# The exchange of the rotation's halves: four ScalarE copies out of PSUM, or four transfers within SBUF on the product with the sine

## The chip, the cores and the metric

The kernel runs on one core of a Trainium2 chip. The metric is the device time of one execution in microseconds (us), the median of the runs. TensorE (PE) multiplies matrices into the eight PSUM banks, VectorE (DVE) and ScalarE (ACT) do the elementwise work, GpSimd (POOL) splits weights, and SyncE (SP) issues the transfers that bring weights in.

## The reference, cut to what matters

Two blocks run one after the other on 512 positions of width 1024. The first has two layers: differential attention (16 query and key heads of 64 numbers) and windowed attention with grouped keys (16 query heads, 4 key heads), each followed by a gated feed-forward part with a convolution and by a gated embedding. The second block joins a convolution branch with an attention branch. The change touches the rotation of queries and keys in the two attentions of the first block:

```python
def apply_rope(x, cos, sin):
    xf = x.astype(jnp.float32)
    x1, x2 = jnp.split(xf, 2, axis=-1)
    c, s = cos[:, :, None, :], sin[:, :, None, :]
    return jnp.concatenate([x1 * c - x2 * s, x2 * c + x1 * s], axis=-1).astype(x.dtype)
```

Heads lie along partitions, two heads of 64 to a tile of 128 partitions and 512 positions. The halves x1 and x2 of a head are 32 partitions each, so the sine term needs each block of 32 partitions moved to its neighbour's place.

## The kernel before, in words

All matrix products are made three times over (high part by high part, high by low, low by high) from operands split into two parts. Weights come as 328 slabs of 512 KB in a fixed order. For each slab SP loads `raw` (2 slots), ACT copies it to `whi` (4 slots), POOL writes the rest to `wlo` (two instructions), PE uses it for 24 products of 128x512, and `slab_done` lets ACT take the slab four further on (`used`). SP works in order: the load of slab s waits on `lo_ready` until slab s-2 has been split.

Every engine's order is the order in which its code is written. The places of this case are `attention(1)` and `attention(2)`. Each has 32 steps (two heads, one block of 128 queries). In step g:

- PE computes the scores of a later step (`scores`, one step ahead in attention 1, two in attention 2), then a part of a query or key projection (`project_qk`; a tile takes two steps in attention 1, three out of four in attention 2), then the transposes of step g's probabilities, and at every second step the outputs (`outputs`) of the two steps before.
- ACT exponentiates (`exps`) the next step, copies the transposes (`prob_high`), copies a rotated tile (`q_high`), now and then empties the output bank, and where a projection tile has finished takes the next slab (`used`) and exchanges halves (`swap_halves`).
- DVE takes row maxima (`maxima`) of a later step, rotates a tile (`rope`), splits the tile before (`q_low`), normalises the next step (`normalise`), and splits the transposes (`prob_low`).

`swap_halves` (line 1066) makes four ACT copies of 32x512 from the projection's PSUM bank to `swap` (line 1075). `rope` (line 1553) then makes three DVE instructions: PSUM times the cosine table (line 1563, which frees the bank), `swap` times the sine table, both operands in SBUF (line 1564), and the sum, both in SBUF (line 1567). The sine table carries the sign. `rC` and `rS` are the tables, `qraw` and `swap` have two slots each. All of these and the probabilities lie in the buffer `AR`, which is the name that the trace gives. The scores of a new pair of heads wait for `q_ready`, which `q_low` raises. In attention 1 projection tiles alternate between banks 1 and 0. In attention 2 all but the first use bank 0.

In the lines that the profile shows, scores, projections, outputs and norm sums are all PE L495; transposes are PE L719.

Of the kernel before, what the change touches and what calls it, by code (L numbers as in the profile page):

```python
# [187 lines left out]
def build(nc, xT, pT, posd, wts, par, con, lamd, outT):  # L188
    ctx = ExitStack()
    with ctx:  # L190
# [69 lines left out]
        def f32(a):  # L260
# [38 lines left out]
        rcol_ready, rspread = sem("rcol_ready"), sem("rspread")  # L299
        vhi_ready, pad_ready = sem("vhi_ready"), sem("pad_ready")  # L300
        swap_ready, rope_ready, qhi_ready, q_ready = (
            sem("swap_ready"), sem("rope_ready"), sem("qhi_ready"), sem("q_ready"))
# [99 lines left out]

        BEGUN = {1: {}, 2: {-2: 0, -1: 1}, 3: {-2: 2, -1: 3}}
        NPROJ = {1: 14, 2: 8, 3: 8}
# [54 lines left out]
        @block.sync  # L459
        def _(sp):  # L460
            def load(s, slot, freed):
                if freed is not None:

                    sp.wait_ge(lo_ready, freed)
                sp.dma_start(raw[:, slot, :], wts[s]).then_inc(raw_ready[slot], 16)

            for s in range(4):
                load(s, s % RAWS, s - 1 if s >= RAWS else None)
            with sp.Fori(1, SLABS // 4) as i:
                for j in range(4):  # L470
                    load(4 * i + j, j % RAWS, 4 * i + j - 1)
            for m in range(KC):

                bank, before = tile_of("down2.2", m // 4, m % 4)
                sp.wait_ge(tile_free[bank], before + 2)
                sp.dma_start(outT[:, m, :], X[:, m, :]).then_inc(out_stored, 16)
            sp.wait_ge(out_stored, 16 * KC)
# [498 lines left out]
        def _(act):  # L976
# [89 lines left out]
            def swap_halves(stage, t, n):  # L1066

                if stage not in ("qk1a", "kq2a"):
                    used(stage, 0, t)
                bank, _ = tile_of(stage, 0, t)  # L1070
# [76 lines left out]
            def attention(kind):  # L1147
# [6 lines left out]
                for g in range(steps):  # L1154
# [26 lines left out]
                    if done is not None and kind < 3:  # L1181
                        swap_halves(PROJ[kind], done, place_of(kind, done)[0])
                    if done is not None and kind == 3:
# [103 lines left out]
            values("v1", (1,), 4, T)  # L1287
            swap_halves("qk1", 0, 2)
            q_high(*place_of(1, 0))
            attention(1)  # L1290
# [18 lines left out]
            values("v2", (0,), 0, 256)  # L1309
            swap_halves("kq2", 0, QT0[2] + 2)  # L1310
            exps(2, 0)
            q_high(*place_of(2, 0))
            swap_halves("kq2", 1, QT0[2] + 3)
            attention(2)
# [139 lines left out]
        def _(dve):  # L1454
# [98 lines left out]
            def rope(stage, t, n):  # L1553
# [3 lines left out]

                dve.wait_ge(swap_ready, n + 1)

# [6 lines left out]
                dve.wait_ge(tile_free[bank], before + 2)  # L1566
                tt(qraw[:, b, :], qraw[:, b, :], swap[:, b, :], ALU.add).then_inc(rope_ready, 1)

            def q_low(n, b, which):
# [92 lines left out]
            def attention(kind):  # L1662
# [8 lines left out]
                for g in range(steps):  # L1671
# [5 lines left out]
                    if kind == 3:  # L1677
                        taps(TAPS_A_STEP[g % 4])
                    if kind < 3 and begun is not None:
                        rope(PROJ[kind], begun, place_of(kind, begun)[0])  # L1680
                    if kind < 3 and halfway is not None:
# [16 lines left out]
                    if g + 1 < steps:  # L1698
                        normalise(kind, g + 1)
                    prob_low(kind, g)  # L1700
                    if kind == 2:
                        for c in OSPLIT.get(g, ()):
# [157 lines left out]
            values_low("v1", (1,), T)  # L1860
            rope("qk1", 0, 2)
            q_low(*place_of(1, 0))
            attention(1)
# [16 lines left out]
            for t in range(2):  # L1880
                q_low(QT0[2] + t, 0, 1 - t)
            values_low("v2", (0,), 256)
            maxima(2, 0)
            rope("kq2", 0, QT0[2] + 2)
            attention(2)
# [377 lines left out]
```

## Time and profile before

| What | Value |
|---|---|
| Median of 3 runs | 2182.42 us (2181.17 to 2186.17) |
| The profiled execution's own time | 2183.27 us |
| Its span (first to last instruction) | 2181.3 us |
| Busy: PE, DVE, ACT, POOL | 2081.8, 1251.8, 975.4, 912.7 us |
| Mean granted TensorE clock | 0.977 of full speed |
| Copies of 32x512 by ACT (line 1075) | 104, at 30.9 to 914.9 us |

The profile's times are microseconds from the span's start. In a timeline a row says when an instruction began, how long it (or a run of equal ones) took, and in brackets how long its engine sat idle just before and what released it. Attention 1 runs from about 86 to 262 us, attention 2 from about 784 to 945 us. The row of a PE instruction's length is modelled; the distance between the starts of successive rows is what it costs.

### The profile page before, as it was taken

Reading aid. Unit: us, or ns where it says so; the run is one execution under the profiler, and the core shown is the slowest. Engines: PE = TensorE matmul, PEld = TensorE weight load, DVE = VectorE, ACT = ScalarE, POOL = GpSimd, SP = SyncE. Lnnn points to the kernel's source line nnn. Section 1 sums busy time; section 2 is a strip of 40 time slices with the busy share of each in tenths; the row PEclk is TensorE's granted clock in tenths of the full one; section 3 lists DMA queues with packets and bytes.
Section 4 is the critical chain, followed back from the end, with each engine's and each line's share of the span. In section 5 each row is a group of like instructions: output and inputs, shape, how many; then the busy total and the mean of one; then the engine's idle time right before and its main releaser. Section 6 shows DMA issues by size and latency. Waiting matters only on the chain. (4 is left out here: it accounts for less than half of the span.)

```text
span 2181.3 us, 28619 instructions
## 1 busy us (share of the span) xinstructions
PE 2081.8 (95%) x9896; PEld 1696.5 (78%) x9896; DVE 1251.8 (57%) x1830; ACT 975.4 (45%) x1546; POOL 912.7 (42%) x660
## 2 busy tenths in 40 slices
PE   6999899999999989899999999999979999999999
PEld 5777578888887877778888887777768688888887
DVE  7477756636265668866726357548779664313222
ACT  5577534524245466644524245434642434423222
POOL 4422034545545431134555456344105354445444
PEclk9999799999999989999999999999989999999999
DMA  4211022323223210012222323222102222332223
GB/s 152 78 49 49 20 66 96 100 97 96 97 97 112 82 58 30 30 49 94 99 97 96 100 93 116 87 78 78 40 11 97 77 87 96 97 97 96 96 97 106
DMA packets 49923, 179.53 MB, mean 82 GB/s; under 512 B 5536, under 2 KB 5792, under 8 KB 49824
## 3 DMA queue, kind: packets, MB, share of 16 engines
q1 hardware_dynamic: 48384, 174.09, 24.2%
q10 hardware_dynamic: 1440, 4.08, 0.5%
q8 instruction: 68, 1.11, 0.2%
q14 instruction: 31, 0.25, 0.0%
HBM read 176.05 MB, written 2.10 MB: 82 GB/s over the span
## 5 line engine op out<-in xcount | busy, mean ns | idle before, releaser
L487 POOL TENSOR_TENSOR wlo<-raw,whi 128x512 fp32r<-128x512 f32 x656 | 912.5, 1414 | 1254.2 <-ACT whi L982 1252.8
L495 PE MATMUL PS<-Bhi,whi 128*128 128x512 f32 x2368 | 936.9, 396 | 29.2 <-POOL wlo L487 14.9
L495 PE MATMUL PS<-Blo,whi 128*128 128x512 f32 x2368 | 926.8, 391 | 0.0
L495 PE MATMUL PS<-Bhi,wlo 128*128 128x512 f32 x2368 | 926.7, 391 | 0.0
L982 ACT ACTIVATE whi<-raw 128x1024 fp32r<-128x1024 f32 x328 | 345.8, 1057 | 591.8 <-PE PS L495 521.8
L495 PEld LDWEIGHTS PS<-Bhi,whi 128*128 128x128 f32 x2368 | 447.6, 189 | 139.8 <-issue 30.1
L495 PEld LDWEIGHTS PS<-Bhi,wlo 128*128 128x128 f32 x2368 | 447.4, 189 | 94.8
L495 PEld LDWEIGHTS PS<-Blo,whi 128*128 128x128 f32 x2368 | 448.0, 189 | 90.7 <-issue 0.5
L1465 DVE TENSOR_TENSOR AR<-PS,R 128x512 f32<-128x512 f32 x172 | 116.5, 689 | 241.0 <-PE PS L495 228.9
L1517 DVE TENSOR_TENSOR X<-X,PS 128x512 f32<-128x512 f32 x96 | 65.8, 687 | 232.6 <-PE PS L495 231.8
L1722 DVE SCALAR_TENSOR_TENSOR AR<-AR,par_sb 128x511 f32<-128x511 f32 x88 | 117.0, 1329 | 8.8 <-ACT AR L1205 8.8
L1220 ACT ACTIVATE Bhi<-AR 128x512 f32 x66 | 41.8, 633 | 166.7 <-DVE AR L1738 166.7
L1940 DVE SCALAR_TENSOR_TENSOR AR<-AR,par_sb 128x512 f32<-128x512 f32 x120 | 114.6, 1012 | 0.0
L1725 DVE SCALAR_TENSOR_TENSOR AR<-AR,par_sb 128x511 f32<-128x511 f32 x88 | 106.8, 1213 | 12.9 <-DVE AR L1722 2.9
L1095 ACT ACTIVATE AR<-PS,nmax 128x512 f32<-128x512 f32 (+3 forms) x160 | 93.3, 590 | 42.7 <-DVE nmax L1584 40.7
L1474 DVE SCALAR_TENSOR_TENSOR Blo<-X,par_sb,Bhi 128x512 fp32r<-128x512 f32 x56 | 65.1, 1163 | 40.2 <-ACT Bhi L1003 39.9
L1205 ACT ACTIVATE AR<-AR,par_sb 128x512 f32<-128x512 f32 x88 | 71.0, 807 | 38.5 <-DVE AR L1465 38.5
L1116 ACT ACTIVATE pthi<-PS 128x512 fp32r<-128x512 f32 (+3 forms) x128 | 56.6, 477 | 67.0 <-PE PS L719 66.0
L1481 DVE TENSOR_TENSOR acc<-acc,sq 128x512 f32<-128x512 f32 x64 | 85.1, 1330 | 0.0
L1742 DVE TENSOR_TENSOR Blo<-AR,Bhi 128x512 f32 x66 | 47.1, 714 | 61.5 <-ACT Bhi L1220 61.5
L719 PE MATMUL PS<-constR,AR 128*128 128x128 f32 x368 | 62.0, 300 | 18.6 <-DVE ptlo L1633 13.1
L719 PEld LDWEIGHTS PS<-constR,AR 128*128 128x128 f32 x368 | 46.8, 153 | 39.7 <-DVE AR L1625 17.2
(222 smaller groups left out, 2072.8 us busy)
## 6 DMA issues: line engine op xcount, KB each, us to landing
raw<-in_weights SPq DMA_DIRECT2D x328, 512.0 KB, 3.3
X<-in_xT ACTq DMA_DIRECT2D x4, 512.0 KB, 7.7
out<-X SPq DMA_DIRECT2D x8, 256.0 KB, 3.2
AR<-in_pT ACTq DMA_DIRECT2D x2, 512.0 KB, 3.9
par_sb<-in_parameters ACTq DMA_DIRECT2D x1, 322.0 KB, 4.5
AR<-in_positions ACTq DMA_DIRECT2D x1, 256.0 KB, 9.0
con_sb<-in_constants ACTq DMA_DIRECT2D x1, 206.5 KB, 8.8
AR<-in_lambdas ACTq DMA_DIRECT2D x1, 128.0 KB, 8.7
```

Source lines behind the costliest of these rows:

```text
L487: ins = pool.tensor_tensor(wlo[:, j, c], raw[:, j % RAWS, c], f32(whi[:, j, c]), ALU.subtract)
L495: return pe.matmul(out, w, x, start=start, stop=stop)
L719: last = pe.transpose(PS[:, 2 + n % 2, k * P:k * P + P], source[:, k * P:k * P + P], ident)
L982: act.activation(whi[:, slot, :], raw[:, slot % RAWS, :], ACT.Copy)\
L1095: act.activation(probs(kind)[:, 2 * (g % 2) + s, 0:nb * P], PS[:, score_bank(kind, n), 0:nb * P], ACT.Exp, bias=nmax[:, n % 4:n % 4 + 1], ...
L1205: act.activation(cv[:, 2 * pair + u, :], us[:, 2 * pair + u, :], ACT.Identity, scale=conv_w[:, l, 1, u, bass.ds(q, 1)], bias=conv_w[:, l, ...
L1465: tt(out, PS[:, bank, :], R[:, :], ALU.mult).then_inc(tile_free[bank], 1)
L1481: tt(acc[:, :], acc[:, :], sq[:, slot, :], ALU.add).then_inc(sq_used, 1)
L1517: tt(X[:, m, :], X[:, m, :], PS[:, bank, :], ALU.add)\
L1722: own.step(stt(c[:, 1:T], x[:, 0:T - 1], conv_w[:, l, 0, u, bass.ds(q, 1)], c[:, 1:T], ALU.mult, ALU.add))
L1725: stt(c[:, 0:T - 1], x[:, 1:T], conv_w[:, l, 2, u, bass.ds(q, 1)], c[:, 0:T - 1], ALU.mult, ALU.add).then_inc(conv_done, 1)
L1940: ins = stt(out, src, k, out, ALU.mult, ALU.add)
```

## The change

The tiles `qk1a` and `kq2a` (the first two of each attention) keep the old way. For the 22 others (14 in attention 1, 8 in attention 2) `swap_halves` and `rope` are gone. ACT does only `used`. DVE multiplies PSUM by the sine table into `qraw` (`rope_sin`, in the step in which the projection finishes, after `prob_low`). SP exchanges the halves of that product from `qraw` to `swap` with four transfers of 32x512 (`exchange`), placed in its program ahead of the load of the slab six further on. A step later DVE multiplies PSUM by the cosine table into the same `qraw` and subtracts `swap` (`rope_add`, after `normalise` and ahead of `prob_low`). SP's loop over slabs is written out for the groups of four that hold such an exchange. In attention 1 the first tile's `rope_add` and `q_high` move into step 0.

```diff
+            def exchange(n):
+
+                sp.wait_ge(sin_ready, n - 1 if n < QT0[2] else n - 3)
+
+                sp.wait_ge(rope_ready, n - 1)
+                for to, of in ((0, 32), (32, 0), (64, 96), (96, 64)):
+                    sp.dma_start(swap[to:to + 32, n % 2, :], qraw[of:of + 32, n % 2, :])\
+                        .then_inc(exchanged[n % 2], 16)
+
+            ahead = {SLAB0["qk1"] + j + 6: j + 2 for j in range(NPROJ[1])}
+            ahead.update({SLAB0["kq2"] + j + 6: QT0[2] + 2 + j for j in range(NPROJ[2])})
...
+                    for s in range(4 * at, 4 * at + 4):
+                        if s in ahead:
+                            exchange(ahead[s])
+                        load(s, s % RAWS, s - 1)
...
-        BEGUN = {1: {}, 2: {-2: 0, -1: 1}, 3: {-2: 2, -1: 3}}
+        BEGUN = {1: {-1: 0}, 2: {-2: 0, -1: 1}, 3: {-2: 2, -1: 3}}
...
                     if done is not None and kind < 3:
-                        swap_halves(PROJ[kind], done, place_of(kind, done)[0])
+                        used(PROJ[kind], 0, done)
...
+            def rope_sin(stage, t, n):
+
+                done(stage, 0, t)
+                bank, _ = tile_of(stage, 0, t)
+
+                dve.wait_ge(q_ready, n - 1)
+                dve.wait_ge(qhi_ready, n - 1)
+                tt(qraw[:, n % 2, :], PS[:, bank, :], rS, ALU.mult).then_inc(sin_ready, 1)
+
+            def rope_add(stage, t, n):
+                bank, before = tile_of(stage, 0, t)
+                b = n % 2
+
+                dve.wait_ge(exchanged[b], 64 * (n // 2 if n < QT0[2] else n // 2 - 1))
+                tt(qraw[:, b, :], PS[:, bank, :], rC, ALU.mult).then_inc(tile_free[bank], 1)
+                dve.wait_ge(tile_free[bank], before + 2)
+                tt(qraw[:, b, :], qraw[:, b, :], swap[:, b, :], ALU.subtract).then_inc(rope_ready, 1)
...
-                    if kind < 3 and begun is not None:
-                        rope(PROJ[kind], begun, place_of(kind, begun)[0])
                     if kind < 3 and halfway is not None:
                         q_low(*place_of(kind, halfway))
...
                     if g + 1 < steps:
                         normalise(kind, g + 1)
+                    if kind < 3 and begun is not None:
+                        rope_add(PROJ[kind], begun, place_of(kind, begun)[0])
                     prob_low(kind, g)
+                    if kind < 3 and finished(kind, g) is not None:
+                        t = finished(kind, g)
+                        rope_sin(PROJ[kind], t, place_of(kind, t)[0])
...
             values("v1", (1,), 4, T)
-            swap_halves("qk1", 0, 2)
-            q_high(*place_of(1, 0))
+            used("qk1", 0, 0)
             attention(1)
...
-            rope("qk1", 0, 2)
-            q_low(*place_of(1, 0))
+            rope_sin("qk1", 0, 2)
             attention(1)
...
+            rope_sin("kq2", 0, QT0[2] + 2)
             maxima(2, 0)
-            rope("kq2", 0, QT0[2] + 2)
+            rope_add("kq2", 0, QT0[2] + 2)
+            rope_sin("kq2", 1, QT0[2] + 3)
             attention(2)
```

ACT at the start of attention 1, before: the row of line 982 is the last `used` ahead of it, line 1095 is `exps`, line 1116 `prob_high`, line 1081 `q_high`.

```order
L1063 ACTIVATE Bhi1<-PS,rcol 128x512 x4
L982 ACTIVATE whi<-raw 128x1024 [waits raw_ready0,slab_done]
L1075 ACTIVATE AR<-PS 32x512 [waits rope_ready]
L1075 ACTIVATE AR<-PS 32x512 x3
L1081 ACTIVATE qkhi<-AR 128x512 [waits rope_ready]
L1095 ACTIVATE AR,sum1<-PS,nmax 128x512 [waits max_ready]
L1095 ACTIVATE AR,rsum<-PS,nmax 128x512 [waits max_ready]
L1116 ACTIVATE pthi<-PS 128x4x128 [waits trans_done]
```

The same place in the changed kernel, where its own lines are 1007 (`used`), 1118 (`exps`), 1139 (`prob_high`) and 1104 (`q_high`):

```order
L1088 ACTIVATE Bhi1<-PS,rcol 128x512 x4
L1007 ACTIVATE whi<-raw 128x1024 [waits raw_ready0,slab_done]
L1118 ACTIVATE AR,sum1<-PS,nmax 128x512 [waits max_ready]
L1118 ACTIVATE AR,rsum<-PS,nmax 128x512 [waits max_ready]
L1139 ACTIVATE pthi<-PS 128x4x128 [waits trans_done]
L1104 ACTIVATE qkhi<-AR 128x512 [waits rope_ready]
```

The first exponentials of attention 1's loop no longer stand behind the four copies and the `q_high` of the first tile.

DVE in attention 2, before: from the `prob_low` (line 1633) of the step in which a tile finishes to the `q_low` (line 1571) two steps on. Lines 1581, 1592 and 1596 are `maxima`, lines 1610 to 1625 `normalise`.

```order
L1633 TENSOR_TENSOR ptlo<-PS,pthi 128x2x128 [waits pthi_ready] x2
L1581 TENSOR_REDUCE nmax<-PS 128x1 [waits score_done] x2
L1592 TENSOR_TENSOR nmax<-nmax,nsink 128x2 [waits dve_step]
L1596 TENSOR_TENSOR sdiff<-nmax,nsink 128x2 [waits max_ready]
L1563 TENSOR_TENSOR AR<-PS,AR 128x512 [waits qhi_ready,q_ready,swap_ready]
L1564 TENSOR_TENSOR AR<-AR 128x512
L1567 TENSOR_TENSOR AR<-AR 128x512 [waits tile_free0,dve_step]
L1610 TENSOR_TENSOR rsum<-rsum 128x2 [waits sink_ready,exp_ready]
L1621 RECIPROCAL rinv<-rsum 128x2 [waits dve_step]
L1625 TENSOR_SCALAR AR<-AR,rinv 128x384 [waits dve_step]
L1625 TENSOR_SCALAR AR<-AR,rinv 128x384
L1633 TENSOR_TENSOR ptlo<-PS,pthi 128x2x128 [waits pthi_ready] x2
```

The same stretch of the changed kernel (line 1673 `prob_low`, 1598 `rope_sin`, 1621 to 1636 `maxima`, 1650 to 1665 `normalise`, 1605 and 1607 `rope_add`):

```order
L1673 TENSOR_TENSOR ptlo<-PS,pthi 128x2x128 [waits pthi_ready] x2
L1598 TENSOR_TENSOR AR<-PS,AR 128x512 [waits qhi_ready,q_ready,slab_done]
L1621 TENSOR_REDUCE nmax<-PS 128x1 [waits score_done] x2
L1632 TENSOR_TENSOR nmax<-nmax,nsink 128x2 [waits dve_step]
L1636 TENSOR_TENSOR sdiff<-nmax,nsink 128x2 [waits max_ready]
L1650 TENSOR_TENSOR rsum<-rsum 128x2 [waits sink_ready,exp_ready]
L1661 RECIPROCAL rinv<-rsum 128x2 [waits dve_step]
L1665 TENSOR_SCALAR AR<-AR,rinv 128x384 [waits dve_step]
L1665 TENSOR_SCALAR AR<-AR,rinv 128x384
L1605 TENSOR_TENSOR AR<-PS,AR 128x512 [waits exchanged1]
L1607 TENSOR_TENSOR AR<-AR 128x512 [waits tile_free0]
L1673 TENSOR_TENSOR ptlo<-PS,pthi 128x2x128 [waits pthi_ready] x2
```

There are still three full instructions for a tile. One moved ahead of `maxima`, two moved behind `normalise`, and the instruction that frees bank 0 is now among these two.

SP in the changed kernel, where before a loop held only loads (line 477 is `exchange`, line 466 `load`):

```order
L466 DMA raw<-in_weights 128x1024
L493 REGISTER_ALU
L493 COMPARE_AND_BRANCH
L477 DMA AR<-AR 32x512 [waits rope_ready,sin_ready]
L477 DMA AR<-AR 32x512 x3
L466 DMA raw<-in_weights 128x1024 [waits lo_ready]
```

Each load of these stretches now stands behind four transfers that wait for DVE.

## Rows read from the trace of the kernel before

**Rows 1.** The page, busy time of the engines over the span.

```profile
PE 2081.8 (95%) x9896; PEld 1696.5 (78%) x9896; DVE 1251.8 (57%) x1830; ACT 975.4 (45%) x1546; POOL 912.7 (42%) x660
```

**Rows 2.** Windows: stretch, length, busy us (instructions) by engine, PEclk, DMA share, GB/s.

```profile
95.00:100.00 5.00, 5.00 (x15) 3.49 (x15) 3.70 (x8) 4.92 (x11) 2.52 (x2) 0.66 0.01 3
...
93.00:231.00 138.00, 135.38 (x705) 99.34 (x703) 105.84 (x202) 106.95 (x213) 31.99 (x26) 0.99 0.14 47
231.00:262.00 31.00, 23.94 (x85) 13.28 (x86) 23.69 (x41) 17.97 (x38) 0.86 (x1) 0.80 0.05 17
799.00:921.00 122.00, 109.87 (x740) 91.79 (x740) 101.97 (x286) 75.54 (x223) 15.18 (x12) 0.93 0.10 31
```

**Rows 3.** Timeline of PE at the start of attention 1.

```profile
94.73 0.49 PE L495 MATMUL PS<-qkhi 64*128 64x512 f32 x1 [1.42 <-ACT AR L1095]
```

**Rows 4.** Timeline of ACT at the start of attention 1.

```profile
87.43 2.39 ACT L1075 ACTIVATE AR<-PS 32x512 f32<-32x512 f32 x4
...
93.90 0.69 ACT L1095 ACTIVATE AR<-PS,nmax 128x512 f32<-128x512 f32 x1 [1.36 <-DVE nmax L1584]
```

**Rows 5.** Timeline of DVE in the middle of attention 1.

```profile
151.90 1.29 DVE L1584 TENSOR_REDUCE nmax<-PS 128x1 f32<-128x512 f32 x2 [0.54 <-PE PS L495]
153.57 0.69 DVE L1563 TENSOR_TENSOR AR<-PS,AR 128x512 f32<-128x512 f32 x1 [0.39 <-ACT AR L1075]
...
165.71 0.69 DVE L1563 TENSOR_TENSOR AR<-PS,AR 128x512 f32<-128x512 f32 x1 [2.48 <-ACT AR L1075]
```

**Rows 6.** Timeline of ACT near the end of attention 1's projections.

```profile
234.44 1.28 ACT L1138 ACT_TABLE_LOAD   x1
...
237.64 0.69 ACT L1095 ACTIVATE AR<-PS,nmax 128x512 f32<-128x512 f32 x1
```

**Rows 7.** Timeline of DVE in attention 2, around one finished tile.

```profile
855.52 1.02 DVE L1581 TENSOR_REDUCE nmax<-PS 128x1 f32<-128x384 f32 x2
856.64 0.70 DVE L1592 TENSOR_TENSOR nmax<-nmax,nsink 128x2 f32<-128x2 f32 x1
857.38 1.21 DVE L1596 TENSOR_TENSOR sdiff<-nmax,nsink 128x2 f32<-128x2 f32 x1
858.50 0.68 DVE L1563 TENSOR_TENSOR AR<-PS,AR 128x512 f32<-128x512 f32 x1
...
860.42 0.15 DVE L1610 TENSOR_TENSOR rsum<-rsum 128x2 f32<-128x2 f32 x1
...
861.48 0.75 DVE L1633 TENSOR_TENSOR ptlo<-PS,pthi 128x256 fp32r<-128x256 f32 x2
...
863.19 0.16 DVE L1596 TENSOR_TENSOR sdiff<-nmax,nsink 128x2 f32<-128x2 f32 x1
863.27 0.68 DVE L1571 SCALAR_TENSOR_TENSOR qklo<-AR,qkhi 128x512 fp32r<-128x512 f32 x1
```

**Rows 8.** Timeline of ACT, the same place.

```profile
855.98 2.40 ACT L1075 ACTIVATE AR<-PS 32x512 f32<-32x512 f32 x4
```

**Rows 9.** Timeline of POOL, the same place.

```profile
856.03 2.53 POOL L487 TENSOR_TENSOR wlo<-raw,whi 128x512 fp32r<-128x512 f32 x2 [16.43 <-ACT whi L982]
```

**Rows 10.** Timeline of PE in attention 2.

```profile
801.54 0.76 PE L495 MATMUL PS<-Bhi,whi 128*128 128x512 f32 x1
...
859.12 0.38 PE L495 MATMUL PS<-qkhi 64*128 64x256 f32 x1 [0.94 <-ACT AR L1095]
...
860.41 0.67 PE L495 MATMUL PS<-Bhi,whi 128*128 128x512 f32 x1
...
883.20 0.39 PE L495 MATMUL PS<-qkhi 64*128 64x256 f32 x2 [1.11 <-DVE qklo L1571]
```

**Rows 11.** Transfers by SP: the stores of 256 KB, issue and landing; three issues on the timeline.

```profile
DMA to landing us min/median/max: 2.0/3.2/4.6
...
2159.94 1.33 SPq L476 DMA_DIRECT2D out<-X  x3
```

More of the change, by code:

```diff
@@ L300, in build @@
         vhi_ready, pad_ready = sem("vhi_ready"), sem("pad_ready")
+        sin_ready, exchanged = sem("sin_ready"), [sem(f"exchanged{n}") for n in range(2)]
         swap_ready, rope_ready, qhi_ready, q_ready = (
@@ L468, in _ @@
                 load(s, s % RAWS, s - 1 if s >= RAWS else None)
-            with sp.Fori(1, SLABS // 4) as i:
-                for j in range(4):
-                    load(4 * i + j, j % RAWS, 4 * i + j - 1)
+            def exchange(n):
[6 more added lines that the diff above has]
+            ahead.update({SLAB0["kq2"] + j + 6: QT0[2] + 2 + j for j in range(NPROJ[2])})
+            groups = sorted({s // 4 for s in ahead})
+            at = 1
+            while at < SLABS // 4:
+                if at in groups:
+                    for s in range(4 * at, 4 * at + 4):
+                        if s in ahead:
+                            exchange(ahead[s])
+                        load(s, s % RAWS, s - 1)
+                    at = at + 1
+                else:
+                    end = min([x for x in groups if x > at] + [SLABS // 4])
+                    with sp.Fori(at, end) as i:
+                        for j in range(4):
+                            load(4 * i + j, j % RAWS, 4 * i + j - 1)
+                    at = end
             for m in range(KC):
@@ L1066, in swap_halves @@
             def swap_halves(stage, t, n):
-                if stage not in ("qk1a", "kq2a"):
-                    used(stage, 0, t)
                 bank, _ = tile_of(stage, 0, t)
@@ L1309, in _ @@
             values("v2", (0,), 0, 256)
-            swap_halves("kq2", 0, QT0[2] + 2)
+            used("kq2", 0, 0)
             exps(2, 0)
             q_high(*place_of(2, 0))
-            swap_halves("kq2", 1, QT0[2] + 3)
+            used("kq2", 0, 1)
             attention(2)
@@ L1556, in rope @@
                 b = n % 2
-                dve.wait_ge(swap_ready, n + 1)
+                dve.wait_ge(swap_ready, n + 1 if n < 2 else n - QT0[2] + 3)
                 if n >= 2:
```

## The prediction

> **What bounds the kernel now.** I began with the page: TensorE is busy for 95% of the span [rows 1], so a microsecond counts only if TensorE idles for it or runs it at the low clock. Windows over the two attentions came next, since nothing else is edited. In attention 1's projections (93 to 231 us) TensorE is busy for 135.4 of 138 us, after them for 23.9 of 31 us at a clock of 0.80, and in attention 2 (799 to 921 us) for 109.9 of 122 us at 0.93 [rows 2]. So attention 1 has almost nothing to give while it projects, and attention 2 has 12 us of idle time. Last came the waits of TensorE in each place, and the timelines of ScalarE and VectorE around them.
>
> At the start of attention 1 TensorE waits 1.42 us for exponentials [rows 3]. ScalarE starts these only at 93.90, because the four copies (2.39 us from 87.43) and the first tile's rotation stand in front [rows 4]. The clock then falls: the window 95 to 100 has 0.66 of full speed [rows 2], a mixture of 2.4 and 1.2 GHz after an idle spell.
>
> In the middle of attention 1 VectorE waits 0.39 and 2.48 us for the copies, in turn [rows 5], and TensorE does not wait with it.
>
> In attention 2 each finished tile shows two idle spells of TensorE: 0.94 us for exponentials that stand behind the copies, and 1.11 us for `q_low` [rows 8, 10]. The second depends on VectorE alone, which has no gap from 855.52 to 863.27 [rows 7].
>
> **What is removed from ScalarE.** 22 tiles times four copies, 2.4 us a tile [rows 4, 8], 53 us in all. By the windows ScalarE is not the bound, so most of it is worth nothing. It is worth time in the places above.
>
> *Start of attention 1.* The scores of the next step are done ahead of 91 us, and `exps` follows them at once instead of at 93.90. The 1.42 us should vanish, and with it the fall of the clock: 5 us times 0.34, or 1.7 us. Sum 3.1 us. The lower bound is 0 (another release, VectorE's, comes just as late), the upper 3.8.
>
> *End of attention 1's projections.* The exponentials at 237.64 come behind two table loads, the first at 234.44 [rows 6], and these follow the `q_high` of the last tile. That still waits for the rotation, which now stands behind `normalise`. I take 0, between a loss of 0.3 and a gain of 1.7.
>
> **What is moved on VectorE.** Three full instructions a tile remain (0.6 us each from start to start), so its work does not shrink, but their places change.
>
> *Attention 2, a middle tile* (`g` is the step after the one that finishes it). `rope_sin` comes ahead of `maxima`: 855.5 to 856.1. `maxima` then ends at 857.1. Its two tiny instructions take 0.70 and 1.21 us where they take 0.16 elsewhere [rows 7], and they end at 858.50, when POOL's 2.53 us from 856.03 end [rows 9]. So they should still end at about 858.55, and the sine product has gone in for nothing. What is behind them shrinks by 0.6 us: `normalise` (860.42 to 861.48, so 1.06 us), two instructions of `rope_add`, `prob_low`, `maxima`, `q_low`. `q_low` starts near 862.75 instead of 863.27. The cost: bank 0 is freed behind `normalise`, at 858.55 + 1.06 + 0.6 = 860.2, while TensorE began the next projection at 860.41 [rows 10]. That just fits. Net, 0.5 us for each of the 6 tiles that finish inside the loop, 3.0 us. Bounds: 0 if the tiny instructions slip by the 0.6 us, 2.05 a tile if both spells went.
>
> The Trainium skill ("SBUF — State Buffer", Who interferes with whom) says that a VectorE instruction with two SBUF inputs is shut out by a GpSimd instruction that reads SBUF, and one with a PSUM input is not. The two stretched rows agree with it, and by it the sum stays as it is.
>
> *Attention 2, first tiles.* There `rope` followed `maxima` at once and the next projection started at 801.54 [rows 10]. Now `q_low` (0.6) and `normalise` (1.06) come in between, so it starts up to 1.6 us later. TensorE had about a microsecond of waits right behind it, which covers some. I book a loss of 1.0, between 0 and 1.6.
>
> *Middle of attention 1.* VectorE is busy for 105.8 of 138 us over 13 tiles, which leaves 2.5 us of idle time a tile [rows 2]. `normalise` now waits for the exponentials (about 0.9 us in one step, 0.3 in the other) with no rotation to cover it. That leaves 1.3 us a tile. The outputs wait for `prob_low`, now behind `rope_add`, but by the steps' pace (11 us a tile) it is done some 2 us ahead. I take 0.
>
> **What is added on SyncE.** 88 transfers of 64 KB, 22 times four. The trace of before has no transfer within SBUF and none this small. The nearest are the stores of 256 KB: three issues take 1.33 us, 0.44 each, and one lands 2.0 us after its issue at the least, 3.2 in the median [rows 11]. So the fourth lands 3 x 0.44 + 2.0 = 3.3 us after the sine product, at the median 4.5. I take 3.3, because a quiet queue is the nearest row and the piece is a quarter of it.
>
> The cover in attention 2 is `maxima` to 858.55 and `normalise`: 856.1 to 859.6, 3.5 us. In attention 1 it is `maxima` 1.2, the wait 0.9 and `normalise` 1.1, so 3.2 us, and 1.3 spare. If the fourth lands L us after the product, attention 2 pays 6 x (L - 3.5) and attention 1 pays 13 x (L - 4.5). At 3.3 both are nothing. Queued behind `exchange` on SP is the load of the slab six further. It waits anyway for POOL's split, 2.5 us after ScalarE's copy of the slab, and both start at the same `slab_done`; the four issues end about when that does, and a slab then has a whole tile's time (11 to 19 us) to land. No cost.
>
> **The sum.** 3.1 + 0 + 3.0 - 1.0 + 0 = 5.1 us. The profiled execution took 2183.27 us (span 2181.3 and 2.0 around it), 0.9 above the median of 2182.42, so the profile should come to 2178.2 and the median to 2177.3 us.
>
> **The rivals.**
>
> *The exchange arrives late (slower).* VectorE, which works in order, stands at `rope_add` with `prob_low` and the next `maxima` behind it. The sum turns at L = 4.35: 6 x 0.85 = 5.1. At 4.9 it gives 8.4 + 5.2 - 5.1, 8.5 us slower, 2191. For it speaks the stores' median of 3.2; against it that those queue behind one another and behind loads, and that they are four times as large. The Trainium skill ("SBUF — State Buffer", Can I just issue two DMAs to hit both halves?) says that transfers to separate groups of partitions serialize. If each of the four took a full 2.0 us after the other, L would be 8 and the kernel 67 us slower; but three stores issued within 1.33 us with a largest landing of 4.6 do not look so [rows 11]. Chance 0.2 for slower.
>
> *The gain is lost again in attention 2 (same).* With L between 3.8 and 4.5, or bank 0 freed after TensorE wants it by 0.5 us a tile, its 3.0 us go and the first tiles still cost 1.0. What remains is 3.1 - 1.0 = 2.1: 2180.3 us. A longer single gap can also bring the clock down, 1.7 us each time. For it speaks how closely 860.2 stands to 860.41. Chance 0.3.
>
> *More than forecast.* If the clock of attention 2 (0.93 over 122 us, 8.5 us lost) gains from fewer gaps, some 5 us more: 2172. It is in the forecast's chance.
>
> **Numbers.** Forecast 0.5, its own range 2172 to 2178. A measurement of this kernel tells about 0.2%, or 4.4 us, from no change, so faster means below 2178.0. Faster 0.5, same 0.3, slower 0.2. The range runs from 2171 to 2191.
>
> **What would show it.** Right: no idle spell at TensorE before the third pair of scores of attention 1 and a full clock behind it; ScalarE's `exps` right behind `maxima`; no idle time at `rope_add` for a transfer; `q_low` of attention 2 half a microsecond nearer to its tile's end; landing of the 64 KB transfers near 2.0 us. Wrong: VectorE idle at line 1605 with a transfer as releaser, issues of more than 0.44 us, TensorE waiting for bank 0 at a projection, or a new wait of transposes for `prob_low`.

## The result, and the profile after

The changed kernel took 2189.23 us in the median of 8 runs (2182.72 to 2195.50), the one before 2182.14 us in 8 runs beside it (2179.72 to 2186.27). The ratio is 1.0026, with a 95% interval from 1.0016 to 1.0037: about 6 us slower by the ratio, 7 between the medians, where 2177.3 us and faster was forecast. The profiled execution took 2189.8 us (span 2187.8).

The page, busy time of the engines: ScalarE lost the forecast 53 us of work [rows 1], and the kernel is slower all the same.

```profile
PE 2084.4 (95%) x9896; PEld 1701.2 (78%) x9896; DVE 1253.0 (57%) x1830; ACT 922.8 (42%) x1458; POOL 912.8 (42%) x660
```

Windows of the same stretches as [rows 2]:

```profile
95.00:100.00 5.00, 5.00 (x24) 3.75 (x24) 4.93 (x9) 3.12 (x7) 2.99 (x2) 1.00 0.23 56
93.00:231.00 138.00, 134.80 (x724) 99.85 (x723) 113.91 (x210) 79.93 (x167) 33.34 (x26) 1.00 0.25 75
231.00:262.00 31.00, 26.66 (x86) 15.60 (x85) 24.30 (x42) 16.73 (x36) 0.00 (x0) 0.61 0.00 1
799.00:921.00 122.00, 106.02 (x720) 90.10 (x719) 91.65 (x264) 56.37 (x185) 15.16 (x12) 0.91 0.12 36
```

The start of attention 1 came out as forecast: in 95 to 100 us the clock is 1.00 instead of 0.66. Attention 2 is where the kernel is worse: TensorE is busy for 106.0 of 122 us instead of 109.9, at 0.91 instead of 0.93.

TensorE and ScalarE at the start of attention 1, in place of [rows 3, 4]: ScalarE's exponentials start at 90.56 instead of 93.90, and the scores at 93.11 wait for nothing.

```profile
93.11 0.50 PE L520 MATMUL PS<-qkhi 64*128 64x512 f32 x2
```

```profile
90.56 0.69 ACT L1118 ACTIVATE AR<-PS,nmax 128x512 f32<-128x512 f32 x1 [3.28 <-DVE nmax L1624]
```

The waits of TensorE over the whole kernel (total us, times, longest). The first row is new, and it is bank 0: line 1605 is the cosine product that frees it. The last row was 11.4 us before.

```profile
PE PS L520 <- DVE AR L1605: 17.2, 6, 3.4
...
PE PS L520 <- ACT AR L1118: 2.6, 2, 1.7
```

Around one tile of attention 2, VectorE, in place of [rows 7] (1598 `rope_sin`, 1621 to 1636 `maxima`, 1665 `normalise`, 1605 and 1607 `rope_add`, 1611 `q_low`):

```profile
854.24 0.68 DVE L1598 TENSOR_TENSOR AR<-PS,AR 128x512 f32<-128x512 f32 x1
854.84 1.01 DVE L1621 TENSOR_REDUCE nmax<-PS 128x1 f32<-128x384 f32 x2
...
857.68 0.75 DVE L1665 TENSOR_SCALAR AR<-AR,rinv 128x384 f32<-128x384 f32 x2
859.51 0.69 DVE L1605 TENSOR_TENSOR AR<-PS,AR 128x512 f32<-128x512 f32 x1 [1.08 <-DMA AR<-AR]
...
862.64 0.69 DVE L1611 SCALAR_TENSOR_TENSOR qklo<-AR,qkhi 128x512 fp32r<-128x512 f32 x1
```

SyncE's queue there, and the summary of all 88 transfers (issue time min/median/max in ns; then us to landing):

```profile
854.95 3.09 SPq L477 DMA_DIRECT2D AR<-AR  x4
858.08 0.58 SPq L466 DMA_DIRECT2D raw<-in_weights  x1
```

```profile
L477 SPq DMA_DIRECT2D AR<-AR x88: 507/591/2050, 86.9 to 918.7; - x88
...
DMA to landing us min/median/max: 1.9/2.0/3.8
```

TensorE there, in place of the 860.41 of [rows 10]:

```profile
860.35 0.47 PE L520 MATMUL PS<-Bhi,whi 128*128 128x512 f32 x1 [2.66 <-DVE AR L1605]
```

The landing of 2.0 us was right. The issue was not: 0.59 us in the median, and the four of this tile take 3.09 us (the second of them alone 1.27). The sine product ends at about 854.9, the fourth transfer lands just ahead of 859.51: L is 4.6 us, not 3.3. VectorE stands still for 1.08 us, and TensorE for 2.66.

**Two yardsticks.** The profile's executions differ by some us in stages that no kernel here touches, so I also read each place by itself, from the starts of ScalarE's copies of weight slabs (there are 328 in a fixed order). *Stretch* is the time from the copy of the 115th slab to that of the 127th, which holds all of attention 2. *Period* is the time from one projection tile of its middle to the next. Before: stretch 190.0 us (766.3 to 956.3), period 19.0 to 19.3. After: 197.2 us (763.0 to 960.2), period 20.2 to 21.0:

```profile
853.69 1.06 ACT L1007 ACTIVATE whi<-raw 128x1024 fp32r<-128x1024 f32 x1
873.92 1.06 ACT L1007 ACTIVATE whi<-raw 128x1024 fp32r<-128x1024 f32 x1
894.63 1.06 ACT L1007 ACTIVATE whi<-raw 128x1024 fp32r<-128x1024 f32 x1
```

So the changed kernel is 3.3 us ahead when it comes to attention 2 (763.0 against 766.3), and 3.9 behind when it leaves it.

The stretch is the coarser yardstick. Its last part, from the 126th copy to the 127th, comes when the last tile has been projected, and takes 43.8 to 47.4 us in the kernels below (without e6_split and e7_double) though only the last tile's rotation is left in it. With one profile of each kernel, stretches that lie less than 3 us apart show little. So the table also has the time from the 121st copy to the 126th, which is five periods.

### The profile page after: what moved, and what is told of

The parts are those of the page before. It is cut to its first block and busy times, and to the rows that moved or that the text cites. A ratio compares the mean times of both kernels' runs of the same rounds, so it can differ in the third digit from the quotient of the medians.

```text
span 2187.8 us, 28555 instructions
## 1 busy us (share of the span) xinstructions
PE 2084.4 (95%) x9896; PEld 1701.2 (78%) x9896; DVE 1253.0 (57%) x1830; ACT 922.8 (42%) x1458; POOL 912.8 (42%) x660
## 3 DMA queue, kind: packets, MB, share of 16 engines
q8 instruction: 68, 1.11, 0.2%
## 5 line engine op out<-in xcount | busy, mean ns | idle before, releaser
L520 PE MATMUL PS<-Bhi,whi 128*128 128x512 f32 x2368 | 936.4, 395 | 47.0 <-DVE AR L1605 17.2
L1785 DVE TENSOR_TENSOR Blo<-AR,Bhi 128x512 f32 x66 | 47.1, 714 | 61.5 <-ACT Bhi L1243 61.5
```

The lines of the kernel that those rows point to most:

```text
L520: return pe.matmul(out, w, x, start=start, stop=stop)
```

## The experiments

All ratios are to the kernel before, with their 95% intervals.

| Kernel | Ratio | Stretch, us | Period, us | 121st to 126th copy, us |
|---|---|---|---|---|
| before | 1 | 190.0 | 19.0 to 19.3 | 95.3 |
| changed | 1.0026 (1.0016 to 1.0037) | 197.2 | 20.2 to 21.0 | 102.7 |
| e1_att1 | 0.9989 (0.9975 to 1.0003) | 189.6 | 19.0 to 19.2 | 95.2 |
| e2_att2 | 1.0042 (1.0026 to 1.0058) | 195.8 | 19.1 to 21.6 | 101.1 |
| e3_nodma | 0.9986 (0.9974 to 0.9997) | 189.7 | 18.4, the last 19.2 | 92.7 |
| e4_earlycos | 1.0018 (1.0005 to 1.0030) | 196.1 | 20.4 to 20.6 | 102.5 |
| e5_latesub | 1.0039 (1.0025 to 1.0053) | 196.1 | 20.3 to 20.7 | 102.2 |
| e6_split | 1.0217 (1.0200 to 1.0234) | 213.0 | 22.0 to 23.5 | 112.6 |
| e7_double (two runs) | 1.0275 (1.0255 to 1.0295) | 217.7 | 23.4 to 24.0 | 118.4 |
| e8_cos_nodma | 0.9970 (0.9959 to 0.9981) | 187.8 | 18.24 | 91.2 |
| e9_sinfirst | 0.9983 (0.9973 to 0.9993) | 185.9 | 18.2 to 18.4, the first 19.8 | 93.0 |
| e10_delay | 1.0004 (0.9995 to 1.0014) | 194.4 | 20.5 to 20.7, the first 19.0 | 101.2 |
| e11_traffic | 0.9983 (0.9973 to 0.9994) | 185.9 | 18.2 to 18.4, the first 19.8 | 92.9 |
| e12_after_sinfirst | 1.0000 (0.9989 to 1.0010) | 189.5 | 18.4 to 19.4 | 94.4 |

### Each attention alone

e1_att1: attention 2 goes back to the copies and `rope`.

```diff
-            ahead.update({SLAB0["kq2"] + j + 6: QT0[2] + 2 + j for j in range(NPROJ[2])})
```

> The exchange by transfers is kept in attention 1 alone (14 tiles); attention 2 is as in the kernel before. Theory (the loss lies wholly in attention 2, where the one bank for projection tiles is freed too late, while the start of attention 1 gains what was forecast): the second step of scores in attention 2 begins at about 780.8 us against 784.1 before, attention 2 takes what it took before, and the whole is 2.5 to 4 us faster than the kernel before (ratio about 0.9985). Rival (the transfers slow every place they are used in, through the longer issues on SyncE or through the traffic): also slower than before, ratio 1.000 or above.

e2_att2: attention 1 goes back to them.

```diff
-            ahead = {SLAB0["qk1"] + j + 6: j + 2 for j in range(NPROJ[1])}
```

> The exchange by transfers is kept in attention 2 alone (8 tiles); attention 1 is as in the kernel before. Theory: TensorE waits 2.6 to 3.4 us at each of six projection tiles for bank 0, attention 2 is 9 to 10 us longer, ratio to the kernel before about 1.0043. Rival (loss spread over both places): about half of the changed kernel's loss, ratio 1.001 to 1.002.

Attention 1 alone gives 0.9989, in the median 2 us faster, though the interval just holds 1. Attention 2 alone gives 1.0042, as expected, with a stretch 5.8 us longer where 9 to 10 were expected. The loss lies in attention 2. That attention 1 gains is shown better by its own pace: two of its projection tiles take 22.0 us from copy to copy in the kernel before and in e2_att2, and 20.9 to 21.2 in the changed kernel and in e1_att1 (the first pair apart). More on this below.

### Without transfers, in the same places

e3_nodma: `exchange` and the wait for it are left out.

```diff
-                dve.wait_ge(exchanged[b], 64 * (n // 2 if n < QT0[2] else n // 2 - 1))
```

> The changed kernel without its 88 transfers and without VectorE's waits for them; the exchange of halves is left out, so that swap holds what it held, and all else stays in its place. It separates the place of the instructions from the time of the transfers. Theory (in attention 2 both count: of a bank wait of 2.66 us about 1.1 is the late transfer, about 1.6 the place of the cosine product behind normalise): the bank wait falls to about 1.6 us a tile, but does not go, and the kernel is 5 to 8 us faster than the changed kernel, 0 to 2 us faster than the one before. Rival A (only the transfers' lateness matters): no bank wait is left and the kernel comes to about the forecast, 2177 us or less. Rival B (only the place matters, and the transfer is hidden in it): within 2 us of the changed kernel.

TensorE in e3_nodma, the same tile. The bank wait is 1.46 us, as expected, and `q_low` costs another 0.74.

```profile
856.07 0.47 PE L509 MATMUL PS<-Bhi,whi 128*128 128x512 f32 x1 [1.46 <-DVE AR L1593]
...
857.53 0.82 PE L733 MATMUL PS<-constR,AR 128*128 128x128 f32 x6
859.09 0.39 PE L509 MATMUL PS<-qkhi 64*128 64x256 f32 x2 [0.74 <-DVE qklo L1599]
```

The stretch is 189.7 us, 0.3 below the kernel before and 7.5 below the changed one. But the 0.3 hides two things. Up to the 126th copy e3_nodma is 3.1 us faster than the kernel before, 2.7 of it in the five periods. Then its last part takes 47.1 us instead of 44.3, and e8_cos_nodma has 47.4 there; in both the granted clock is 0.66 in the window 935 to 945 us, and 0.83 in the kernel before. So placement alone does gain while tiles are projected. The transfers then cost 10.0 us in five periods (102.7 against 92.7), 2.0 a tile.

The wait does not account for that. TensorE idles 2.66 us a tile in the changed kernel, and 1.46 + 0.74 = 2.20 in e3_nodma. Most of the rest is the clock, 0.91 in 860 to 880 us of the changed kernel and 1.00 there in e3_nodma. In the changed kernel the products behind the long wait start 0.23 us apart at first, then 0.42:

```profile
861.61 0.63 PE L520 MATMUL PS<-Bhi,wlo 128*128 128x512 f32 x1
862.03 1.48 PE L744 MATMUL PS<-constR,AR 128*128 128x128 f32 x6
863.45 0.59 PE L520 MATMUL PS<-qkhi 64*128 64x256 f32 x2
```

### Bank 0 freed early

e4_earlycos: `rope_cos`, right behind `maxima` in attention 2, frees the bank; `rope_add` is only the subtraction.

```diff
+            def rope_cos(stage, t, n):
+                bank, before = tile_of(stage, 0, t)
+                tt(sq[:, n % 2, :], PS[:, bank, :], rC, ALU.mult).then_inc(tile_free[bank], 1)
...
+                    tt(qraw[:, b, :], sq[:, b, :], swap[:, b, :], ALU.subtract).then_inc(rope_ready, 1)
```

> In attention 2 the cosine product goes into a buffer of its own (sq, free there) right behind maxima, where the rotation stood before, and frees bank 0 there; only the subtraction waits for the transfers, behind normalise. Transfers and their number are as in the changed kernel. Theory: TensorE's waits for bank 0 in attention 2 (six of 2.6 to 3.4 us) go, VectorE still idles about 0.5 to 1 us a tile for the transfer and q_low is no earlier than in the kernel before, so attention 2 comes back to about its time before, and with the gain of attention 1 the kernel is 2 to 5 us faster than the one before. Rival (the late transfer itself holds the chain through q_low and the probabilities, whatever the bank does): less than 3 us faster than the changed kernel, still at or above the one before.

My theory failed here, and the rival came true. The waits for bank 0 shrank from 17.2 to 3.0 us, and the stretch by only 1.1. VectorE idles just 0.59 us a tile for the transfer, ahead of the subtraction:

```profile
855.97 0.69 DVE L1611 TENSOR_TENSOR AR<-sq,AR 128x512 f32<-128x512 f32 x1 [0.59 <-DMA AR<-AR]
```

TensorE now waits in other places of the same chain, 1.04 us for `prob_low` and 1.12 for `q_low`:

```profile
857.14 0.85 PE L744 MATMUL PS<-constR,AR 128*128 128x128 f32 x6 [1.04 <-DVE ptlo L1682]
859.11 0.56 PE L520 MATMUL PS<-qkhi 64*128 64x256 f32 x2 [1.12 <-DVE qklo L1620]
```

e8_cos_nodma is e4_earlycos without transfers.

> The kernel with the cosine product behind maxima in attention 2, without its 88 transfers and without the waits for them; the exchange of halves is left out. With the kernel without transfers before it, it gives the price of the cosine product's place where no transfer is late. Theory: no waits for bank 0 and none for transfers, the stretch between the 115th and 127th slab copies is 187 to 189 us, against 189.9 without transfers in the place of the changed kernel: the place is worth 1 to 3 us. Rival (place is worth nothing, VectorE's chain is as long either way): 189.5 to 190.5.

Its stretch is 187.8 us, 8.3 below e4_earlycos, and its five periods are 11.3 us shorter. Six tiles with 0.59 us of idle time are 3.5 us. So lateness costs more than its length, or the transfers cost in another way too.

### Subtraction later, and two queues

e5_latesub moves the subtraction behind `prob_low`.

```diff
+                    prob_low(kind, g)
+                    if kind == 2 and begun is not None:
+                        rope_add(PROJ[kind], begun, place_of(kind, begun)[0])
```

> As the last one (cosine product into a buffer of its own behind maxima in attention 2), and the subtraction there moved behind prob_low, so that the transfers have about a microsecond more to land. Theory now (in attention 2 TensorE follows VectorE's chain, and what counts is the time in which VectorE stands and waits for the fourth transfer; where the bank is freed is a lesser part): VectorE waits for no transfer in attention 2, the stretch between the copies of the 115th and the 127th weight slab by ScalarE, 190.0 us before and 197.2 in the changed kernel, is 188 to 190.5, and the kernel is 2 to 4 us faster than the one before. Rival (the transfers cost by more than their wait, for instance by slowing other work): it stays at 194 us or more, slower than before.

Within attention 2's loop VectorE waits for a transfer for 0.3 us in all (and 2.3 once ahead of it), and the stretch stays at 196.1. Another miss. TensorE now meets one spell of 1.87 us, and the projection behind it takes 3.52 us (840.05 to 843.57), against 2.19 for the same nine products in e8_cos_nodma (858.48 to 860.67):

```profile
838.79 0.38 PE L520 MATMUL PS<-qkhi 64*128 64x256 f32 x1 [1.87 <-DVE qklo L1620]
...
840.05 0.79 PE L520 MATMUL PS<-Bhi,whi 128*128 128x512 f32 x1
```

e6_split issues two of each tile's four transfers from ScalarE.

```diff
+            def exchange_act(n):
+                act.wait_ge(sin_ready, n - 1 if n < QT0[2] else n - 3)
+                act.wait_ge(rope_ready, n - 1)
+                for to, of in ((64, 96), (96, 64)):
+                    act.dma_start(swap[to:to + 32, n % 2, :], qraw[of:of + 32, n % 2, :])\
+                        .then_inc(exchanged[n % 2], 16)
```

> The changed kernel with two of each tile's four transfers issued by ScalarE and two by SyncE, side by side; nothing else moves. If the issues (0.59 us each, one after the other) are the late part, the fourth lands 1.2 us earlier, VectorE's wait of 1.08 us at rope_add in attention 2 goes, TensorE's wait for bank 0 falls from 2.7 to about 1.6 us and the stretch between the 115th and 127th slab copies from 197.2 to about 191 us; the kernel is 4 to 7 us faster than the changed one. Rival (the two queues still complete one after the other, or ScalarE's own issues delay its exponentials by as much): less than 2 us faster.

It is 2.2% slower. ScalarE works in order: it waits for the sine product and issues for 1.87 us, and its slab copy and the exponentials stand behind that.

```profile
864.44 1.87 ACTq L1105 DMA_DIRECT2D AR<-AR  x2
866.41 1.06 ACT L1007 ACTIVATE whi<-raw 128x1024 fp32r<-128x1024 f32 x1 [3.11 <-issue]
```

So the run says nothing on two queues as such, only that this engine can't spare the time.

### The price of the issues

e7_double: eight transfers of 16 partitions a tile.

```diff
+                for to, of in ((0, 32), (16, 48), (32, 0), (48, 16), (64, 96), (80, 112), (96, 64), (112, 80)):
+                    sp.dma_start(swap[to:to + 16, n % 2, :], qraw[of:of + 16, n % 2, :])\
```

> The changed kernel with eight transfers of 16 partitions a tile in place of four of 32: same bytes, twice the issues. If each issue costs 0.59 us whatever its size, the last lands 2.4 us later, at L of about 7.0 us in attention 2 and 6.3 in attention 1. By the prediction's own cost formula with these L attention 2 grows by 6 x 2.4 = 14 us against the changed kernel and attention 1 by 13 x (6.3 - 4.5) = 23 us at most; TensorE then waits in attention 1 too. Rival (the issue's time goes with the bytes, 0.3 us for 32 KB): L unchanged, within 2 us of the changed kernel.

The issue costs the same at half the size, and VectorE's wait grows by 2.3 us, as expected:

```profile
866.26 5.44 SPq L477 DMA_DIRECT2D AR<-AR  x8
```

```profile
873.10 0.69 DVE L1605 TENSOR_TENSOR AR<-PS,AR 128x512 f32<-128x512 f32 x1 [3.35 <-DMA AR<-AR]
```

The stretch grew by 20.5 us, where six times 2.4 is 14; 4.4 of it lie behind the 126th copy, and the five periods grew by 15.7, 3.1 a tile. In attention 1 the 31st slab's copy begins at 324.9 us against 296.2 in the changed kernel, 28.7 us where at most 23 were expected. The mechanism holds, and the price per microsecond of lateness is higher than one.

### Lateness without transfers, transfers without lateness

e10_delay adds one VectorE instruction to e8_cos_nodma.

```diff
+                    own.step(tt(swap[:, b, :], swap[:, b, :], rS, ALU.mult))
+                    own.wait()
```

> No transfers at all; the kernel without transfers and with the cosine product behind maxima (e8), plus one more VectorE instruction of 128x512 (0.6 us, swap times the sine table into swap) ahead of the subtraction of each tile of attention 2. The exchange of halves is left out. It puts the lateness of the transfers, 0.6 us, in without any transfer. Theory: the tile's period grows from 18.24 to about 20 us, by three times the 0.6 us, since TensorE's clock falls behind the longer idle spell, and the stretch between the 115th and 127th slab copies from 187.9 by 7 to 11 us. Rival (the loss is the transfers' traffic): the stretch grows by 3.6 us (6 x 0.6) at most, the clock stays full in the middle of attention 2.

e11_traffic has all transfers, and nobody needs them.

```diff
+                    sp.dma_start(swap[to:to + 32, n % 2, :], rC[of:of + 32, :])\
...
+                    landed(n - 1)
...
+                    tt(qraw[:, b, :], sq[:, b, :], rS, ALU.subtract).then_inc(rope_ready, 1)
```

> The opposite: the 88 transfers are issued at the same points of SyncE's program with the same sizes, but read the cosine table, and nothing near them waits for them (a tile waits for the transfers of the tile before, long landed). The subtraction takes the sine table in place of the exchanged halves, so the rotation's sine term is not the true one. Theory: traffic costs nothing, the tile's period stays at 18.2 to 18.4 us and the stretch between the 115th and 127th slab copies within 1 us of the 187.9 without transfers. Rival: 194 us or more, as with the true transfers.

These two settle it. With no transfer at all, 0.6 us more on VectorE brings the stretch from 187.8 to 194.4 us (6.6, just under the 7 to 11 expected) and the period from 18.24 to 20.5. With all the traffic and no lateness, the stretch is 185.9 and four of the five periods are 18.2 to 18.4.

The fifth, the first of them, took 19.8 us in e11_traffic, at a clock of 0.91, and 18.24 in e8_cos_nodma at 1.00. TensorE's waits just ahead are the same in both (0.41, 0.36 and 1.11 to 1.12 us). So the length of the waits alone does not decide when the clock falls; what else does, no run here shows. In e10_delay it fell in all but the first.

TensorE in e8_cos_nodma, one tile: the waits, and the nine products of the next projection, at 0.23 us from start to start.

```profile
855.79 0.85 PE L733 MATMUL PS<-constR,AR 128*128 128x128 f32 x6 [0.36 <-DVE ptlo L1669]
857.76 0.39 PE L509 MATMUL PS<-qkhi 64*128 64x256 f32 x2 [1.11 <-DVE qklo L1607]
...
858.48 0.50 PE L509 MATMUL PS<-Bhi,whi 128*128 128x512 f32 x1
...
860.67 0.60 PE L733 MATMUL PS<-constR,AR 128*128 128x128 f32 x4
```

The same in e10_delay:

```profile
856.45 0.85 PE L733 MATMUL PS<-constR,AR 128*128 128x128 f32 x6 [1.08 <-DVE ptlo L1671]
858.42 0.39 PE L509 MATMUL PS<-qkhi 64*128 64x256 f32 x2 [1.11 <-DVE qklo L1609]
...
859.18 0.80 PE L509 MATMUL PS<-Bhi,whi 128*128 128x512 f32 x1
...
861.05 0.63 PE L509 MATMUL PS<-Blo,whi 128*128 128x512 f32 x1
861.48 0.63 PE L509 MATMUL PS<-Bhi,wlo 128*128 128x512 f32 x1
...
862.87 0.82 PE L733 MATMUL PS<-constR,AR 128*128 128x128 f32 x6
```

One wait is longer, 1.08 instead of 0.36 us. The nine products then take 3.69 instead of 2.19 us, most of them 0.43 us from start to start: TensorE runs those at 1.2 instead of 2.4 GHz. Of the 2.26 us by which the period grew, 0.72 is the wait and 1.50 the clock. Windows of 20 us in mid attention 2, first e8_cos_nodma, then e10_delay (the third number from the end is the granted clock):

```profile
860.00:880.00 20.00, 18.11 (x134) 15.33 (x133) 16.66 (x52) 9.89 (x33) 2.53 (x2) 1.00 0.08 27
```

```profile
860.00:880.00 20.00, 17.39 (x120) 14.48 (x120) 15.38 (x45) 8.83 (x31) 2.53 (x2) 0.93 0.09 27
```

The Trainium skill ("TensorE: Matmul & The Clock Gate", "Wait — 56ns, not 53.3ns?") gives 426.7 ns from start to start for 512 columns at the low clock and 215.7 at the high one. The rows of e10_delay agree with the first, at 0.43; those of e8_cos_nodma have 0.23, a little above the second.

### The sine product earlier

e9_sinfirst is e4_earlycos with `rope_sin` ahead of `prob_low` in attention 2; e12_after_sinfirst is the changed kernel with that edit alone.

```diff
+                    if kind == 2 and finished(kind, g) is not None:
+                        t = finished(kind, g)
+                        rope_sin(PROJ[kind], t, place_of(kind, t)[0])
                     prob_low(kind, g)
```

> As the kernel with the cosine product behind maxima in attention 2 (e4), and rope_sin there moved ahead of the prob_low of its step, where VectorE idles 0.49 us for ScalarE's copy of the transposes. Theory (a wait of VectorE for the transfers of 0.6 us a tile lengthens TensorE's idle spells a little and then costs the clock too, 1.3 us more a tile; without lateness neither is paid): the transfers start about 1.1 us earlier, VectorE waits for none of them in attention 2, the tile's period falls from 20.3 to about 18.5 us, the stretch between the 115th and 127th slab copies from 196.1 to 188 to 190 us, and the kernel is 3 to 6 us faster than the one before. Rival (transfers slow attention 2 by being there, late or not): the period stays at 20 us or more and the kernel at or above the one before.

> The changed kernel with one edit: in attention 2 rope_sin stands ahead of the prob_low of its step. The cosine product stays behind normalise. Theory: the transfers land about in time (1.1 us earlier against a wait of 1.08), the wait for bank 0 falls from 2.66 to about 1.5 us as without transfers, and the stretch between the 115th and 127th slab copies from 197.2 to 190 to 191.5 us; the kernel is 4 to 7 us faster than the changed one, and from 1 us slower to 3 us faster than the one before. Rival (the prob_low that is now later costs TensorE as much): less than 3 us faster than the changed one.

VectorE in e9_sinfirst: the sine product goes into an idle spell, and the subtraction here waits for nothing.

```profile
846.10 0.68 DVE L1598 TENSOR_TENSOR AR<-PS,AR 128x512 f32<-128x512 f32 x1
846.71 0.74 DVE L1682 TENSOR_TENSOR ptlo<-PS,pthi 128x256 fp32r<-128x256 f32 x2
...
852.05 0.68 DVE L1611 TENSOR_TENSOR AR<-sq,AR 128x512 f32<-128x512 f32 x1
```

e9_sinfirst beats both kernels: 2179.5 us in the median beside 2183.77, ratio 0.9983 (0.9973 to 0.9993), with a stretch of 185.9 us and the full clock in 840 to 900 us. e12_after_sinfirst, which adds and removes nothing and only moves one VectorE instruction, has a ratio of 1.0000 where the changed kernel has 1.0026, and a stretch of 189.5 us in place of 197.2. VectorE waits for transfers there for 0.5 us in all, instead of 7.1. What still lies between e12_after_sinfirst and e9_sinfirst is the place of the cosine product: the first waits 10.8 us for bank 0 in attention 2, the other 3.0.

## Why the prediction was wrong

Two steps failed above all: the issue time of a transfer, 0.44 us where it is 0.59 and more, and a microsecond of lateness priced at one microsecond where it cost about two. The parts of the sum, one by one:

- **Start of attention 1, +3.1 us: right in kind, too large.** The idle spell and the fall of the clock are gone. At the 18th slab's copy, two tiles on, the changed kernel is 2.2 us ahead (116.0 against 118.2).
- **Middle of attention 1, 0: wrong.** It gained 3.1 us more by the 28th copy (223.0 against 228.3). The failed step is "attention 1 has almost nothing to give while it projects", taken from TensorE's busy time. Once in each pair of tiles of the kernel before, the exponentials of a step's two heads stand behind the copies and begin 0.67 us apart, and the next scores, whose two halves each wait for one of them, begin 0.67 us apart too. No idle spell shows it. In the changed kernel the two halves start together (x2) and are through 0.65 us sooner, and a pair of tiles takes 21.2 us instead of 22.0. Before, ScalarE and then TensorE:

```profile
165.71 0.69 ACT L1095 ACTIVATE AR<-PS,nmax 128x512 f32<-128x512 f32 x1
166.38 0.68 ACT L1095 ACTIVATE AR<-PS,nmax 128x512 f32<-128x512 f32 x1
```

```profile
166.54 0.49 PE L495 MATMUL PS<-qkhi 64*128 64x512 f32 x1
167.21 0.50 PE L495 MATMUL PS<-qkhi 64*128 64x512 f32 x1
168.09 0.50 PE L495 MATMUL PS<-Bhi,whi 128*128 128x512 f32 x1
```

TensorE in the changed kernel:

```profile
163.63 0.51 PE L520 MATMUL PS<-qkhi 64*128 64x512 f32 x2
164.53 0.50 PE L520 MATMUL PS<-Bhi,whi 128*128 128x512 f32 x1
```

VectorE waits for transfers there, by 0.2 to 0.9 us, which its spare time takes up, and once by 2.14 us; that pair of tiles took 22.6 us.
- **End of attention 1's projections, 0: not shown.** From the 28th copy to the 31st the changed kernel gains 0.8 us, and others with the same attention 1 gain 0.6 to 3.0.
- **What is left of attention 1 at attention 2: 3.3 us, near the forecast 3.1 by luck.** The kernel was 6.1 us ahead at the 31st copy (296.2 against 302.4). Then 2.8 us went back in the feed-forward part, which no edit touches: a wait there is 2.0 instead of 1.1 us, and the window 410 to 430 us has a clock of 0.91 instead of 1.00. Eight other kernels with the new attention 1 lose 2.6 to 3.0 us there too, e11_traffic none; why was not tested. And e2_att2, whose attention 1 is the old one, is also 2.8 us ahead at the 115th copy, so a lead of 3 us at that point proves nothing by itself.
- **Attention 2 without transfers, +3.0 - 1.0: about the right size, by another way.** e3_nodma gained 3.1 us up to the 126th copy, 0.5 a tile in the five periods, and 0.4 instead of -1.0 in the first tiles. The step "that just fits" failed: bank 0 came free 1.46 us too late, not 0.2 too early. The scores ahead of the projection no longer waited for exponentials, so TensorE wanted the bank earlier, about 854.6 in e3_nodma. I had taken its time from a trace in which TensorE was still held up by what the change removes, and in that tile the projection ran at the low clock (0.43 us from start to start) with no wait for `q_low` behind it. What paid for it was that same wait, gone, and the two heads' scores side by side again: they start 0.57 us apart at 859.12 [rows 10] before, and together in e3_nodma.
- **Issue time of a transfer, 0.44 us: the step that turned the sign.** It was 0.59 us in the median, and 3.09 us for the four of a middle tile of attention 2, one of which took 1.27. With the landing of 2.0 us that makes L 4.6. My own formula turns at 4.35, and at 4.6 gives 6 x 1.1 = 6.6 us of loss in attention 2, so 5.1 becomes -1.5: the rival "the exchange arrives late".
- **Lateness costs its own length: wrong.** VectorE's wait of 1.08 us a tile cost 2.0 us a tile in the changed kernel (against e3_nodma), and in e10_delay 0.6 us of lateness cost 2.26 us a tile, 1.50 of it the clock. I had named this ("a longer single gap can also bring the clock down") and put it into no sum.
- **`q_low` half a microsecond nearer: wrong** in the changed kernel, where the 1.08 us of waiting stand ahead of it. Without transfers TensorE's wait for it fell from 1.11 [rows 10] to 0.74 us.
- **SyncE's loads, no cost: right.** The load behind the exchange issues in 0.58 us, and no wait of ScalarE for weights appeared in attention 2.

The sum by stages is 3.3 gained and 7.2 lost, 3.9 us slower at the 127th slab. The profile ends 6.5 us behind. The other 2.6 us arise behind attention 2, where nothing was edited, and were not tested. They are not peculiar to the changed kernel: e1_att1, e3_nodma, e4_earlycos, e5_latesub, e8_cos_nodma, e9_sinfirst, e11_traffic and e12_after_sinfirst each lose 4.5 to 5.1 us on the kernel before between the copies of the 220th and 230th slabs, and e10_delay nothing. How far such places move the medians is open.

## What to carry to other kernels

Where a copy is replaced by a transfer, work out when the last of its transfers lands from issue times of that very kind and count, and compare it with the slack of the engine that waits in order, not with that of the bank or buffer. Do not take a busy TensorE for one with nothing to give: see whether products that can run side by side do so. Before you book a resource as "free in time", ask when it will be wanted once the wait that you remove is gone. Where TensorE already idles about a microsecond twice in a tile, price lateness well above its length, because the clock may go with it (here 0.6 us cost 2.3 a tile, 1.1 us cost 2.0); and look first for an idle spell into which the instruction that starts the transfer can move.

## What the hardware showed that I had not expected

- A transfer of 64 KB within SBUF takes SyncE 0.59 us to issue, one of 32 KB just as long (median 589 ns over 176). A weight load of 512 KB behind four of them takes 0.58 us, and 0.33 in e9_sinfirst. The Trainium skill ("DMA: Bandwidth & Descriptors", "Issuing engines are not separate DMA queues") calls the issue time that a second engine would save "usually small relative to the DMA itself"; here four issues take 2.4 us in attention 1 and 3.1 to 3.9 in attention 2, against a landing of 2.0.
- Two transfers issued by ScalarE took it 1.87 us.
- Transfers to four groups of 32 partitions do not land one after the other: the four issued from 854.95 landed 2.5, 2.7, 2.0 and 2.0 us after their own issues, so the rival with L = 8 is out.
- 88 transfers beside full work on all engines slowed nothing that could be told from the scatter (e11_traffic, stretch 185.9 us, against 187.8 without any; 92.9 against 91.2 in five periods, all of the difference in the first).
